# VectorE takes a share of the weighted sum of gathered expert rows from TensorE

## The reference, cut to what matters

```python
q = (t @ w_query).reshape(T, PEER_HEADS, 2, PEER_HALF)
s = jnp.einsum('thpd,pnd->thpn', q, sub_keys)
top_s, top_i = lax.top_k(s, 16)
cand_s = top_s[:, :, 0, :, None] + top_s[:, :, 1, None, :]     # and cand_i = i0 * 128 + i1
best_s, best_pos = lax.top_k(cand_s, 16)
experts, gates = take(cand_i, best_pos), softmax(best_s)       # 8 heads x 16 = 128 for a token
act = gelu(einsum('td,ted->te', t, expert_u[experts]))
out = einsum('te,ted->td', gates * act, expert_v[experts])
```

## Time and profile before

| | |
|---|---|
| median of 3 runs | 2898.27 us (2896.94 to 2899.92) |
| profiled execution | 2896.53 us, span of its instructions 2894.9 us |
| TensorE matmul busy | 2603.0 us (90%) |
| VectorE busy | 1330.9 us (46%) |
| GpSimd busy | 1097.7 us (38%) |
| ScalarE busy | 495.0 us (17%) |
| DMA | 809.97 MB, 280 GB/s on average, 392 GB/s from 200 to 1870 us |

### The profile page before, as it was taken

One profiled execution on the slowest core, in us unless ns is written; L12 is line 12 of the kernel. 1 busy time (PEld: TensorE's weight loads), 2 busy tenths in 40 slices (PEclk: granted clock), 3 DMA queues, 4 the chain that ended last, 5 costly groups with the idle time before them and its releaser, 6 DMA issues.

```text
span 2894.9 us, 42843 instructions
## 1 busy us (share of the span) xinstructions
PE 2603.0 (90%) x17022; PEld 2274.4 (79%) x17022; DVE 1330.9 (46%) x3785; ACT 495.0 (17%) x1093; POOL 1097.7 (38%) x1033
## 2 busy tenths in 40 slices
PE   7979999889999889999897777689799999979999
PEld 6878889888899888889897777665378876537887
DVE  1246557467467557567467766423521101352110
ACT  1211231110231111232010000013311101331110
POOL 0027556666556676556766777500000000000000
PEclk9989999999999999999998998989699999959999
DMA  7479999999999999999999999722024452202444
GB/s 289 153 278 397 413 393 365 412 371 395 414 407 402 414 381 385 411 400 366 410 352 401 377 398 380 297 94 107 1 87 146 149 214 97 97 1 87 146 155 150
DMA packets 170071, 809.97 MB, mean 280 GB/s; under 512 B 19820, under 2 KB 21904, under 8 KB 153616
## 3 DMA queue, kind: packets, MB, share of 16 engines
q0 software_dynamic: 147936, 539.61, 47.8%
q1 hardware_dynamic: 21792, 267.29, 24.2%
q10 hardware_dynamic: 144, 0.31, 0.0%
HBM read 806.07 MB, written 1.05 MB: 279 GB/s over the span
## 4 chain that ended last, share of the span: by engine, by line
PE 63%; DMA 12%; POOL 10%; DVE 8%; issue 6%; ACT 1%; DVEq 0%; SPq 0%; ACTq 0%; POOLq 0%
PE ea L597 17%; PE pa L614 14%; PE ea L614 13%; DMA vrow<-in_expert_v,idx 11%; PE pa L430 8%; POOL urow L1605 5%; POOL vrow L1605 5%; PE pa L519 4%; DVE rstd L1444 2%; DVE urow L1393 2%; PE pa L438 1%; PE s L456 1%; PE ob L733 1%; PE ob L479 1%; PE s L762 1%
## 5 line engine op out<-in xcount | busy, mean ns | idle before, releaser
L597 PE MATMUL ea<-diag,vrow 128*128 128x128 f32 x8192 | 987.6, 283 | 163.6 <-DMA vrow<-in_expert_v,idx 159.3
L597 PEld LDWEIGHTS ea<-diag,vrow 128*128 128x128 f32 x8192 | 970.7, 200 | 180.5 <-issue 167.2
L1605 POOL DMA_INDIRECT urow<-in_expert_u,idx x512 | 536.2, 1047 | 553.1 <-DVE dots L1393 238.6
L1393 DVE CUSTOM_DVE_ANT_0 urow<-urow,h2n 128x1024 f32<-128x1024 f32 x512 | 604.1, 1221 | 150.7 <-DMA urow<-in_expert_u,idx 146.7
L1605 POOL DMA_INDIRECT vrow<-in_expert_v,idx x512 | 558.2, 1090 | 191.6 <-issue 145.9
L614 PE MATMUL pa<-hT,wring 128*128 128x272 f32 x960 | 235.7, 405 | 23.2 <-DVE hT L1460 23.2
L614 PEld LDWEIGHTS pa<-hT,wring 128*128 128x128 f32 x960 | 188.3, 197 | 66.0 <-DVE hT L1460 24.9
L430 PE MATMUL pa<-hA,wring 128*128 128x128 f32 x2048 | 237.2, 278 | 0.5 <-DVE hA L1186 0.5
L430 PEld LDWEIGHTS pa<-hA,wring 128*128 128x128 f32 x2048 | 234.8, 194 | 1.3 <-issue 1.3
L614 PE MATMUL ea<-hT,wring 128*128 128x272 f32 x960 | 225.1, 393 | 0.0
L614 PEld LDWEIGHTS ea<-hT,wring 128*128 128x128 f32 x960 | 182.2, 190 | 38.3 <-issue 0.8
(11 more groups left out here) (244 smaller groups left out, 2143.1 us busy)
## 6 DMA issues: line engine op xcount, KB each, us to landing
wring<-in_weights SPq DMA_DIRECT2D x126, 2048.0 KB, 8.7
urow<-in_expert_u,idx POOLq DMA_INDIRECT x512, 9.1
vrow<-in_expert_v,idx POOLq DMA_INDIRECT x512, 10.0
area<-in_const POOLq DMA_DIRECT2D x1, 1544.0 KB, 6.8
xT<-in_x SPq DMA_DIRECT2D x1, 1024.0 KB, 5.7
out_x<-xT SPq DMA_DIRECT2D x1, 1024.0 KB, 4.6
cols<-in_cols POOLq DMA_DIRECT2D x2, 274.0 KB, 7.7
urow<-bias_scratch POOLq DMA_DIRECT2D x1, 512.0 KB, 6.6
```

The lines of the kernel that those rows point to most:

```text
L597: m = pe.matmul(EA[c // 4][:, (c % 4) * P:(c % 4 + 1) * P], vrow[:, b, c * P:(c + 1) * P], diag[:, b, :], start=False, stop=final and c % ...
L1393: dve.tensor_tensor_reduce(out=urow[:, b, :], in0=urow[:, b, :], in1=h2n[:, u % 2, :], scale=1.0, scalar=0.0, op0=ALU.mult, op1=ALU.add, a ...
L1605: pool.indirect_dma_start(out=rows[:, b, :], out_offset=None, in_=table, in_offset=bass.IndirectOffsetOnAxis(ap=idx[:, k % 2, col:col + 1] ...
```

## The change

- `SUMMED = (1, 1, 1, 2)`: of the four v rows of a group, VectorE sums the last one, in the last unit the last two. TensorE and the diagonals have the other three, or two (`PE_ROWS`).
- `sum_rows`: `acc = row * w + acc` with w the token's weight, one instruction over 128 x 1024 for each row; the first of a unit writes `acc` without adding. It stands on VectorE behind the dot products of the next group and waits for the row's landing. Each counts up `e_acc`.
- TensorE adds `acc` at the end of a unit: eight matmuls with the identity, which transpose it.
- GpSimd waits for `e_acc` too before it gathers v rows into the same buffers.
- `expert_sum` moves from ahead of the first scaling of the next unit to behind that group's diagonals.
- To make room for `acc`, `eqw` is halved: `best_experts` works on each of the two heads in turn, six instructions of 800 elements in place of three of 1600. `diag` has room for six matrices instead of eight.

```diff
+SUMMED = (1, 1, 1, 2)
+PE_ROWS = [GB - SUMMED[q // GROUPS_TILE] for q in range(UNITS * GROUPS_TILE)]
...
+                        for i in range(PE_ROWS[q]):
...
+                        if g == GROUPS_TILE - 1:
+                            pe.wait_ge(e_acc, summed_rows(q + 1))
+                            for c in range(KC):
+                                m = pe.matmul(EA[c // 4][:, (c % 4) * P:(c % 4 + 1) * P], acc[:, c * P:(c + 1) * P], ident,
+                                              start=not by_rows, stop=not by_rows or c % 4 == 3)
...
+                for h in range(2):
+                    estep(tt_(eq, iota.unsqueeze(1).to_broadcast([P, TOPK, CAND]),
+                              bestf[:, h, :].unsqueeze(2).to_broadcast([P, TOPK, CAND]), ALU.is_equal))
+                    esettle()
+                    estep(tt_(eq, eq, cidx[:, h, :].unsqueeze(1).to_broadcast([P, TOPK, CAND]), ALU.mult))
+                    esettle()
+                    estep(dve.tensor_reduce(idxf[:, TOPK * h:TOPK * h + TOPK], eq, AX.X, ALU.add))
+                    esettle()
...
+            def sum_rows(q):
+
+                for i in range(PE_ROWS[q], GB):
+                    b, w = GB * (q % 2) + i, wgt[:, q % 2, i:i + 1]
+                    n = summed_rows(q) + i - PE_ROWS[q]
+                    dve.wait_ge(v_full[b], 16 * (q // 2 + 1))
+                    if n:
+                        dve.wait_ge(e_acc, n)
+                    if n == summed_rows(q // GROUPS_TILE * GROUPS_TILE):
+                        if q:
+                            dve.wait_ge(e_x, 2 * (q // GROUPS_TILE))
+                        m = dve.tensor_scalar(acc[:], vrow[:, b, :], w, None, ALU.mult)
+                    else:
+                        m = stt(acc[:], vrow[:, b, :], w, acc[:], ALU.mult, ALU.add)
+                    m.then_inc(e_acc, 1)
...
                         if g == 0:
                             pair_gates(k)
-                            if k and k % PAIRS == 0:
-                                expert_sum(u - 1)
-                        dve.wait_ge(gelu_done, k * GROUPS + g + 1)
+                        if q:
+                            sum_rows(q - 1)
+                        dve.wait_ge(gelu_done, q + 1)
...
-                        for i in range(GB):
-                            b = GB * (g % 2) + i
-                            dve.tensor_scalar(diag[:, b, :], ident, wgt[:, g % 2, i:i + 1], None, ALU.mult)\
+                        for i in range(PE_ROWS[q]):
+                            dve.tensor_scalar(diag[:, DIAG_SLOTS * (q % 2) + i, :], ident, wgt[:, q % 2, i:i + 1], None, ALU.mult)\
                                .then_inc(diag_done, 1)
+                        if q and q % GROUPS_TILE == 0:
+                            expert_sum(u - 1)
...
-                    pool.wait_ge(v_free, GB * (q - 1))
+                    pool.wait_ge(v_free, rows_used(q - 1))
+                    pool.wait_ge(e_acc, summed_rows(q - 1))
```

More of the change, by code:

```diff
@@ L80, with pe_rows, summed_rows, rows_used @@
 TURNS_E = UNITS * PAIRS
+GROUPS_TILE = PAIRS * GROUPS
+SUMMED = (1, 1, 1, 2)
+PE_ROWS = [GB - SUMMED[q // GROUPS_TILE] for q in range(UNITS * GROUPS_TILE)]
+DIAG_SLOTS = max(PE_ROWS)
+def pe_rows(n):
+    return sum(PE_ROWS[:n])
+def summed_rows(n):
+    return GB * n - pe_rows(n)
+def rows_used(n):
+    return pe_rows(n) + (n - 1) // GROUPS_TILE
 SLOT = ([0, 1, 2, 3, 4, 5, 6, 7] + [8 + i // 2 for i in range(MAPS + 2)]
@@ L169, in program @@
             vrow = sb("vrow", [P, UB, D])
-            diag = sb("diag", [P, UB, P])
+            diag = sb("diag", [P, 2 * DIAG_SLOTS, P])
+            acc = sb("acc", [P, D])
             h2n = sb("h2n", [P, 2, D])
             keys = sb("keys", [P, PAIRS, 512])
-            eqw = sb("eqw", [P, PART * CAND])
-            eq = part(eqw, 0, PART, CAND)
+            eqw = sb("eqw", [P, TOPK * CAND])
+            eq = part(eqw, 0, TOPK, CAND)
             work, junk = part(eqw, 0, 4, P), part(eqw, 512, 128)
@@ L245, in program @@
         u_free, v_free = sem("u_free"), sem("v_free")
-        gelu_done, gate_exp = sem("gelu_done"), sem("gate_exp")
+        gelu_done, gate_exp, e_acc = sem("gelu_done"), sem("gate_exp"), sem("e_acc")
         diag_done, e_step, e_gmax, e_idx, e_key, e_x = (sem(n) for n in (
@@ L586, in experts @@
                         pe.wait_ge(e_x, 2 * u)
-                    for n in range(2):
-                        pe.matmul(EA[n][:], ident, zeros, start=True, stop=False)
-                    for g in range(PAIRS * GROUPS):
-                        for i in range(GB):
+                    by_rows = SUMMED[u] < GB
+                    if by_rows:
+                        for n in range(2):
+                            pe.matmul(EA[n][:], ident, zeros, start=True, stop=False)
+                    for g in range(GROUPS_TILE):
+                        q = u * GROUPS_TILE + g
+                        for i in range(PE_ROWS[q]):
                             b = GB * (g % 2) + i
[L592 to L595, removed]
+                            pe.wait_ge(diag_done, pe_rows(q) + i + 1)
+                            pe.wait_ge(v_full[b], 16 * (q // 2 + 1))
                             for c in range(KC):
                                 m = pe.matmul(EA[c // 4][:, (c % 4) * P:(c % 4 + 1) * P], vrow[:, b, c * P:(c + 1) * P],
-                                              diag[:, b, :], start=False, stop=final and c % 4 == 3)
+                                              diag[:, DIAG_SLOTS * (q % 2) + i, :], start=False, stop=False)
+                            m.then_inc(v_free, 1)
+                        if g == GROUPS_TILE - 1:
[3 more added lines that the diff above has]
+                                              start=not by_rows, stop=not by_rows or c % 4 == 3)
                             m.then_inc(v_free, 1)
@@ L1379, in expert_sum @@
             def expert_sum(u):
-                dve.wait_ge(v_free, SLOTS * (u + 1))
+                dve.wait_ge(v_free, pe_rows((u + 1) * GROUPS_TILE) + u + 1)
                 for hf in range(2):
@@ L1395, in experts @@
                                                      accum_out=dots[:, g % 2, i:i + 1]).then_inc(u_free, 1)
+                        q = k * GROUPS + g
                         if g == 0:
                             pair_gates(k)
-                            if k and k % PAIRS == 0:
-                                expert_sum(u - 1)
-                        dve.wait_ge(gelu_done, k * GROUPS + g + 1)
-                        if k or g >= 2:
-                            dve.wait_ge(diag_done, k * PART + GB * (g - 1))
+                        if q:
+                            sum_rows(q - 1)
+                        dve.wait_ge(gelu_done, q + 1)
+                        if q >= 2:
+                            dve.wait_ge(diag_done, pe_rows(q - 1))
                         estep(tt_(wgt[:, g % 2, :], gl[:, g % 2, :], gates[:, GB * g:GB * g + GB], ALU.mult))
                         esettle()
-                        if k or g >= 2:
-                            dve.wait_ge(v_free, k * PART + GB * (g - 1))
-                        for i in range(GB):
-                            b = GB * (g % 2) + i
-                            dve.tensor_scalar(diag[:, b, :], ident, wgt[:, g % 2, i:i + 1], None, ALU.mult)\
+                        if q >= 2 and PE_ROWS[q]:
+                            dve.wait_ge(v_free, rows_used(q - 1))
+                        for i in range(PE_ROWS[q]):
+                            dve.tensor_scalar(diag[:, DIAG_SLOTS * (q % 2) + i, :], ident, wgt[:, q % 2, i:i + 1], None, ALU.mult)\
                                .then_inc(diag_done, 1)
+                        if q and q % GROUPS_TILE == 0:
+                            expert_sum(u - 1)
                         if k + 1 < TURNS_E:
@@ L1418, in experts @@
                         yield
+                sum_rows(TURNS_E * GROUPS - 1)
                 expert_sum(UNITS - 1)
```

## The result

The changed kernel takes 2920.8 us (median of 4, 2917.2 to 2926.4) against 2899.1 us for the kernel before: ratio 1.0076, interval 1.0058 to 1.0095. It is slower by 22 us (17 to 28 by the interval). The forecast was 2906 us, slower, with 2875 to 2938 as the range.

The account below looks back on a forecast made before the run. DMA was taken to bound most of the expert stretch, TensorE its dips, GpSimd's gather issue the last unit. Relief -18 - 7 - 1, picking +0.6, slower gathers +21 + 12 gave +7.6 on 2898.3: 2906 us, range 2875 to 2938.

Parts of the forecast that it names:

- A: In two TensorE-bound stretches, 400 to 480 and 1260 to 1360 us, less TensorE work gains 18 us (9 to 21).
- B: Before the keys, at three unit ends, TensorE's shorter chain through a group's rows gains 7 us (0 to 11).
- C: At the kernel's end, TensorE finishes sooner after the last row lands, a gain of 1 us.
- E: First three units, where GpSimd waits for nothing: sums lengthen gathers' issue in 24 groups, +12 us (0 to 24).
- D: Last unit, about 27 groups with two sums: the sums lengthen gathers' issue, +21 us (4 to 39).
- one group traced: Last unit: late dot products after two sums delay gathers by 0.48 and 1.04 us; net 1.43 us a group, 39 in all.
- The prediction's other figure for D, 29 us: Last unit, by the skill's shared-port rule: gathers starting at any moment of a sum lose 0.53 us per sum.
- I cost the wait itself at nothing: First three units: VectorE's wait for the previous group's row holds nothing TensorE has not, so 0 us.
- The rival of the full VectorE: Last unit: VectorE becomes the bound, dot products run back to back and gathers wait for them; +35, 2933 us, chance 0.22.
- the upper bound: Last unit: the highest cost of the sums to gathers' issue, 1.43 us a group, 39 us in all.
- The rival on the other side: Sums lock in phase with landings and cost gathers 0.14 us a group; faster by 20, 2878 us, chance 0.32.

Follow-up runs that it names:

- The kernel with both operands in PSUM: The changed kernel with the last unit's accumulator and the tokens' vector of its dot products moved to PSUM: 2890.7 us, 0.9979 against the kernel before.
- kernel without the sums: The changed kernel with the rows VectorE sums gathered but added by nobody, no sum waits, no accumulator; computation incomplete: 2873.1 us, 0.9922 against the kernel before.
- The wait alone: The kernel before plus VectorE's wait for the last v row of the group before, no sum: 2912.8 us, 1.0044 against the kernel before.

## Why the prediction was right, and where it was not

The direction and the range held; the size did not. +7.6 us was forecast and +21.7 measured, in a range of 63 us, with 0.47 on slower. In the prediction's own terms the profiled executions give -18.3 (A and B) - 1 (C) + 11.4 (E) + 27.7 (the last unit), in all +19.8. So the 12 us that were missing came half from TensorE's relief, 25 forecast and 18.3 seen, and half from D, 21 forecast and 27.7 seen.

1. What bounds the last unit: right. GpSimd's issue sets its pace: 0.96, 1.06 and 1.17 us for a gather go with 330.7, 347.2 and 374.9 us between the marks (the first of these in the kernel before with the dot products in PSUM). The kernel with both operands in PSUM has 0.95 and 340.3, since its gathers also wait for dot products. The signs named for this held, or nearly: 1.15 us was forecast for a gather and 1.17 measured, 0.30 apart, with TensorE busy for 51% where under 50% was forecast.
2. Terms A, B and C, TensorE's relief: -26 forecast, -22.6 measured by the kernel without the sums. That the totals are so near is partly luck. Up to the first mark A and B bring 18.3 instead of 25. Another 3.3 us come in the last unit, which was to gain nothing, and from the last mark to the write of x that kernel takes 22.2 us, where C had 26.7: it adds no sums there. The sign named for A also failed: in 400 to 480 us the changed kernel has 361 GB/s and TensorE at 95%, not 400 and under 90%. The kernel without the sums has 381 GB/s and 97% there. C shows by itself in the changed kernel: from the first u gather of the last group to the write of x it was 27.7 us before and is 26.7, 1 us less as worked out.
3. Term E, what the sums give back in the first three units: +12 forecast, 11.4 between the traces, and up to 18 by the spread of the first mark. That the two sides there cancel almost wholly, as the medians of the kernel without last-unit sums say, was not forecast: A, B and E left 13 us.
4. Term D, the last unit: mis-sized, +21 forecast, 27.7 against the kernel before and 31.0 against the kernel without the sums. It was the middle, 0.79 us a group, between sums that stay in phase and one group traced, 1.43. Spread over its 27 groups the measured cost is 1.03 to 1.15 us, in the upper half. The mechanism of the traced end was right: dot products that start late and back to back behind the sums. The prediction's other figure for D, 29 us, is near by luck: it counts only gathers that meet a sum, and those lost 9.9 us.
5. "I cost the wait itself at nothing": wrong. The argument looked at what TensorE gets later, nothing, and not at when the dot products start. The wait alone costs 0.4%.
6. The rival of the full VectorE: its load was right (232.76 of 285 us, 93% forecast in 1620 to 1680 and 90% measured), its consequence not: in 1557 to 1842 us gathers waited only 0.6 us for dot products. The rule behind the upper bound, that gathers wait for the end of a running instruction, carried the loss: an excess of 55.9 us instead of 28.9 in the table.
7. The rival on the other side, sums in phase with landings, fell with the timeline above.

Hardware, in the prediction's own terms: what lengthens a gather is, nearly always, an instruction of VectorE with two long SBUF operands. In the kernel before, from 1540 to 1870 us, all 27 gathers of 1.2 us or more began during one. One that started 0.04 us after such an instruction took 1.04 us longer, and those that started in one of the picking's two 1600-element steps with two operands took 0.6 to 0.8 us longer; none did in a dot product with one operand in PSUM. One instruction with a single long SBUF operand did it too: the first sum of a unit, 0.75 us, which writes `acc` without adding. In the changed kernel a gather that began 0.34 us after its start, at 1088.21 us, took 1.20 us. The Trainium skill (SBUF — State Buffer, section Who interferes with whom) says that a VectorE instruction with two SBUF inputs contends with a GpSimd instruction that reads SBUF, and one with at most one SBUF input, outside the 2-port perf modes, does not. The runs agree for the dot products and the adding sums: with their long operands in PSUM the mean is 0.95 to 0.96 us. A gather here reads its row numbers from SBUF (`idx`). In which mode the 0.75 us instruction ran, no run shows.

What stays open: how the wait's 0.4% divides between the units, since its profiled execution, 7 us longer in the last unit and 3 us ahead at the first mark, shows only about half of it. Of the last unit's 27.7 us the wait alone gives 7 in its trace, and gathers that begin during a sum are 10. How the rest arises from the sum's length and from what it pushes back was not separated.

## What to carry to other kernels

Where gathers are issued back to back by GpSimd, look at the mean and the shortest of their issue. Here the difference was time lost to VectorE instructions with two SBUF operands, and moving one operand to PSUM got it back. It needed two free banks and one copy of the tokens' vector. An instruction added to VectorE can cost more by where it puts the next long instructions than by what it holds up itself, here 18 us against 10; cost a new wait by what starts late behind it, not only by who waits for its result. Relief for the busiest engine is worth what the dips below the next limit hold, here 23 us for 309 us of work.

## What was not expected of the hardware

- One sum of 1.29 us in a group cost the last unit as much as two: gathers of 1.17 us on average in both.
- TensorE's granted clock fell with its load: 0.70 of full speed in 1557 to 1842 us with 51% busy, where it was 0.92 with 76%. 32 matmul records, two rows, took up to 6.74 us there, where 64 had mostly taken 7.38 before. Two rows still fitted into a group of 11.8 us, and gathers waited 1.5 us for TensorE in that stretch.
- A sum that reads and writes its accumulator in PSUM takes 1.29 us, the same as in SBUF.
